# A layer stack on one core: weights, x and the scratch region moved onto 512-byte boundaries of each partition

## What is computed

```python
def _swiglu(h, w_gu, w_down):
    g, u = jnp.split(h @ w_gu, 2, axis=-1)
    return (jax.nn.silu(g) * u) @ w_down
...
x = x + 0.5 * _rmsnorm(_swiglu(_rmsnorm(x, ffn1_pre_g), ffn1_w_gu, ffn1_w_down), ffn1_post_g)
h = _rmsnorm(x, mix_pre_g)
q, k, v, z, xbc, dt_raw, gate_logits = jnp.split(h @ w_in, cuts, axis=-1)
...
mixed = (g_attn * attn_out + g_ssd * ssd_out) @ w_mix_out
x = x + _rmsnorm(mixed, mix_post_g)
```

## Time and profile before

| | |
|---|---|
| median of 3 runs | 1121.41 us (1120.94 to 1121.94) |
| profiled execution: time, span | 1121.69 us, 1119.9 us |
| TensorE busy | 1104.4 us, 99% |
| VectorE, ScalarE busy | 793.0 us, 590.9 us |
| granted clock | 1.00 |
| read from HBM | 186.50 MB |

### The profile page before, as it was taken

How to read it: one execution, slowest core, us unless ns; L and a number is a source line. 1 busy time by engine, 2 the same in 40 slices (tenths; PEclk the granted TensorE clock), 3 DMA queues, 4 the chain that set the end, 5 groups by cost and what they waited for, 6 DMA issues and landing times.

```text
span 1119.9 us, 20894 instructions
## 1 busy us (share of the span) xinstructions
PE 1104.4 (99%) x8484; PEld 1042.5 (93%) x8484; DVE 793.0 (71%) x1112; ACT 590.9 (53%) x844; POOL 0.2 (0%) x4
## 2 busy tenths in 40 slices
PE   9999999999999999999999999999999999999998
PEld 8999999999999999999999898999999799999998
DVE  5755555858898977777777867665555686987774
ACT  5444444557664325586744555443443575664561
POOL 0000000000000000000000000000000000000000
PEclk9999999999999999999999999999999999999999
DMA  8665555455544236444555434355555345543341
GB/s 298 241 222 187 190 184 188 168 183 180 185 151 148 94 136 207 155 147 151 188 174 177 169 114 160 131 200 206 173 176 206 128 166 198 184 151 114 114 151 38
DMA packets 29137, 188.59 MB, mean 168 GB/s; under 512 B 3496, under 2 KB 4809, under 8 KB 7370
## 3 DMA queue, kind: packets, MB, share of 16 engines
q1 hardware_dynamic: 26592, 181.42, 46.8%
q10 hardware_dynamic: 2474, 6.15, 1.7%
HBM read 186.50 MB, written 1.05 MB: 167 GB/s over the span
## 4 chain that ended last, share of the span: by engine, by line
PE 79%; DVE 15%; ACT 4%; issue 2%; DVEq 0%; ACTq 0%
PE bank L500 23%; PE bank L502 23%; PE bank L501 23%; DVE sb_w_lo L1973 4%; PE bank L581 2%; DVE sb_ssd_conv L2196 1%; ACT sb_w_hi L1287 1%; PE bank L816 1%; PE bank L961 1%; PE bank L655 1%; PE bank L1033 0%; PE bank L1012 0%; DVE sb_ssd_xdt L2243 0%; DVE sb_hyF L2626 0%; DVE sb_hyF L2625 0%
## 5 line engine op out<-in xcount | busy, mean ns | idle before, releaser
L1973 DVE TENSOR_TENSOR sb_w_lo<-sb_w_raw,sb_w_hi 128x2048 fp32r<-128x2048 f32 x169 | 386.5, 2290 | 156.9 <-ACT sb_w_hi L1287 156.7
L500 PE MATMUL bank<-sb_hT_hi,sb_w_hi 128*128 128x256 f32 x1560 | 442.7, 284 | 1.4 <-DVE sb_hT_lo L2050 1.3
L502 PE MATMUL bank<-sb_hT_hi,sb_w_lo 128*128 128x256 f32 x1560 | 435.3, 279 | 0.0
L501 PE MATMUL bank<-sb_hT_lo,sb_w_hi 128*128 128x256 f32 x1560 | 435.2, 279 | 0.0
L1287 ACT ACTIVATE sb_w_hi<-sb_w_raw 128x2048 fp32r<-128x2048 f32 x169 | 322.4, 1908 | 36.3 <-PE bank L502 34.9
L500 PEld LDWEIGHTS bank<-sb_hT_hi,sb_w_hi 128*128 128x128 f32 x1560 | 292.2, 187 | 6.0 <-issue 3.6
L501 PEld LDWEIGHTS bank<-sb_hT_lo,sb_w_hi 128*128 128x128 f32 x1560 | 291.8, 187 | 2.4 <-issue 1.2
L502 PEld LDWEIGHTS bank<-sb_hT_hi,sb_w_lo 128*128 128x128 f32 x1560 | 292.3, 187 | 0.0
L1341 ACT ACTIVATE sb_ffn_gate<-sb_ffn_gate 128x256 f32<-128x256 f32 x44 | 18.4, 418 | 140.7 <-DVE sb_ffn_gate L2065 140.7
L500 PE MATMUL bank<-sb_w_hi,sb_hT_hi 128*128 128x256 f32 x256 | 73.2, 286 | 0.6 <-DVE sb_hT_lo L2725 0.3
L501 PE MATMUL bank<-sb_w_lo,sb_hT_hi 128*128 128x256 f32 x256 | 71.1, 278 | 0.0
(11 more groups left out here) (431 smaller groups left out, 1751.3 us busy)
## 6 DMA issues: line engine op xcount, KB each, us to landing
sb_w_raw<-in_w SPq DMA_DIRECT2D x169, 1024.0 KB, 5.0
sb_x<-in_x SPq DMA_DIRECT2D x2, 512.0 KB, 4.6
sb_w_raw<-in_w SPq DMA_DIRECT2D x4, 256.0 KB, 7.0
sb_w_raw<-in_w SPq DMA_DIRECT2D x2, 512.0 KB, 8.2
sb_mem_xn<-in_mem ACTq DMA_DIRECT2D x1, 1024.0 KB, 7.8
sb_post_g<-in_ffn_post_g ACTq DMA_DIRECT2D x2, 512.0 KB, 4.6
sb_decay<-in_c_decay ACTq DMA_DIRECT2D x1, 768.0 KB, 4.3
out<-sb_x SPq DMA_DIRECT2D x3, 256.0 KB, 2.2
```

The costliest lines, as they stand in the source:

```text
L500: pe.matmul(o, a_hi, b_hi, start=first, stop=False)
L501: pe.matmul(o, a_hi, b_lo, start=False, stop=False)
L502: return pe.matmul(o, a_lo, b_hi, start=False, stop=last)
L1973: tt(w_lo[b % STAGES][:], w_raw[b % RING][:], f32(w_hi[b % STAGES][:]), ALU.subtract).then_inc(w_lo_in, 1)
```

## The change

Six small tensors are allocated ahead of the weights, `hT_hi` and `hT_lo` come right behind x, the other small tensors behind them, and 64 bytes that nobody uses (`to_row`) end the list. No instruction is added, removed or moved; each works on the same tensors at other addresses.

```diff
+ROW_GAP = 16
...
+        strict_r = sb("strict_r", [P, P], F32R)
+        newton = sb("newton", [P, 3, 16])
+        rstd = sb("rstd", [P, 16])
+        m_ssq = sb("m_ssq", [P, TOK * MLA_HEADS])
+        xr = sb("xr", [P, TOK])
+        xa_r = sb("xa_r", [P, TOK])
+
         w_raw = [sb(f"w_raw{i}", [P, BLOCK]) for i in range(RING)]
         w_hi = [sb(f"w_hi{i}", [P, BLOCK], F32R) for i in range(STAGES)]
         w_lo = [sb(f"w_lo{i}", [P, BLOCK], F32R) for i in range(STAGES)]
         x = sb("x", [P, TOK, D])
+        hT_hi = sb("hT_hi", [P, KD, SEQ], F32R)
+        hT_lo = sb("hT_lo", [P, KD, SEQ], F32R)
         square = sb("square", [P, 6 * P])
         cols = sb("cols", [P, NCOLS])
-        strict_r = sb("strict_r", [P, P], F32R)
         fcols = sb("fcols", [FILTER_HIDDEN, 4])
         rows = sb("rows", [P, NROWS])
         sub_g = sb("sub_g", [P, 1])
-        newton = sb("newton", [P, 3, 16])
         ssq = sb("ssq", [P, TOK])
...
-        m_ssq = sb("m_ssq", [P, TOK * MLA_HEADS])
-        rstd = sb("rstd", [P, 16])
-        xr = sb("xr", [P, TOK])
-        xa_r = sb("xa_r", [P, TOK])
         post_eps = sb("post_eps", [P, TOK])
-        hT_hi = sb("hT_hi", [P, KD, SEQ], F32R)
-        hT_lo = sb("hT_lo", [P, KD, SEQ], F32R)
+        sb("to_row", [P, ROW_GAP])
```

## The result

| | before | after |
|---|---|---|
| median of 4 runs each | 1121.53 us (1120.94 to 1121.94) | 1134.99 us (1134.89 to 1135.19) |
| ratio, 95% interval | | 1.0121 [1.0103, 1.0138] |
| profiled execution: time, span | 1121.69, 1119.9 us | 1134.89, 1133.1 us |

The forecast was 1109.5 us, with a range up to 1124.5. The time lies 13.5 us on the other side of before, and outside the range.

The account below looks back on a forecast made before the run. TensorE was taken to bound the kernel, with 79% of the chain. From the profiled 1121.69 us, 12 for faster split products and 0.1 for transfers gave 1109.6, against the median 1109.3; forecast 1109.5 us, range 1098 to 1124.5.

Parts of the forecast that it names:

- the bound of TensorE's split products: Split-product matmuls on TensorE: at best 23.6 us gained, at worst 6.6 us lost, nothing if only the starting phase decides.
- the value taken: Feature blocks get the token blocks' share of fast products, 68% for 9%: 14.1 us, 12 after losses where VectorE limits.
- The 512-column products: 528 products with 512 moving columns, left at 233.3 ns each; a gain, which nothing showed, would be 3.5 us.
- both operands on one footing is the worse footing: Rival: equal offsets make weight load and matmul collide, token blocks lose their fast cadence; 1125.7 to 1128 us, chance 0.23.
- The argument against it: Transposes of x have both operands alike within a row, yet last as long as the others.
- VectorE's 2290 ns: The 169 roundings on VectorE, mean 2290 ns each, were to stay unchanged.
- transfers: Loads hidden in the ring; only first x and last result could gain, 0.1 us taken, 0.4 at most.
- damped where other engines are the limit: Some 2 us of the products' gain lost where VectorE limits, 320 to 410 us and pauses at 900 us.
- the worse case: The layout makes split products slower: chance 0.23, of which a third was to stay below 1124.5 us.
- token blocks at 118 ns or a third cadence above it: Sign in the product starts that the change made the kernel worse, instead of feature blocks at 113.3 ns for 117.8.
- The rule of the Trainium skill: Loading next weights takes no read bandwidth from the running matmul, so their place wouldn't matter; only the ends' 0.1 us remains.

Follow-up runs that it names:

- e3: Kernel before with weights, hT and region all moved by 384 bytes, their offsets against each other unchanged: 1122.02 us, ratio 1.0001.
- e5: Kernel before with only a 448-byte pad ahead of hT_hi, operand offsets equal modulo 256, neither on a 512-byte boundary: 1134.84 us, ratio 1.0117.
- e1: Kernel before with pads that put weights and x on a 512-byte boundary, hT and region left at 448: 1112.91 us, ratio 0.9921.
- e4: Kernel before with only a 128-byte pad ahead of hT_hi, weights left at 128, hT and region at 64: 1115.15 us, ratio 0.9933.
- e7: e1 with the feed-forward halves that stand in 512-column blocks moved 64 bytes onto the weights' offset: 1119.28 us, ratio 0.9968 to the kernel before.
- m3_types: Matmul stretches without the layers, in three types at various operand offsets: float32 216 ns and bf16 109.2 ns at every offset; only fp32r varied.
- the map: Fp32r matmul stretches without the layers, each with other operand offsets: 256 columns took 120.0 ns at equal offsets, 113.3 and 117.8 at difference 192.

## Why the prediction was wrong

**The step that failed** is the bound of TensorE's split products: "Worst: all 1,475 products at the short cadence take the long one, 6.6 us more." It began with a true remark, that no row has both operands on a boundary, and then took the two cadences that the trace shows for the only ones there are. The trace had split products at D = 64 and 192 only; equal offsets give a third cadence, 120.0 ns, and it costs the 5,316 products of the long cadence too. Measured, the 256-column products cost 20.4 us more, where 6.6 had been called the worst.

**Its neighbour, the value taken,** failed with it. The 68% of the token blocks were read as "the moving operand lies better". e3 and e5 show that where an operand lies is nothing by itself. D = 192 for the feature blocks does make them faster: e1 has 66% of them short, near the token blocks' 68%, and its time falls by 8.6 us. But e4, with the same D, had 38% in its profile and e7 35%, so that the share came out is partly chance; and the layout that it was applied to had another D.

**The 512-column products,** "I leave them there", stood at 233.3 in all of the trace because it had one D for them. They fell to 227.9, 3.1 us of gain that the sum left out.

**The rival** *both operands on one footing is the worse footing* was the right mechanism at 0.23, mis-sized by the same bound: it priced only the loss of the short cadence, at 4.3 to 6.6 us, where the products cost 17.3 net and the time 13.5. The argument against it came from transposes in full precision, a type that m3_types shows to be indifferent.

**Right:** VectorE's 2290 ns; ScalarE; transfers, with landings of 4.9 and 4.4 us for 5.0 and 4.6, of which the 4.9 stands in e5 too, whose weights lie off the boundary; that a change in the products is damped where other engines are the limit. That was put at 2 us and was 4.1, 1.2 of them at the places named (320 to 410 us and around 900). Of what was to show the worse case the text named "token blocks at 118 ns or a third cadence above it", and it was the third cadence.

**The rule of the Trainium skill** that was weighed (TensorE: Matmul & The Clock Gate, Step-by-step: what each phase is for), by which loading the next weights takes nothing from the running matmul, would have given no change. The trace doesn't agree for fp32r: with 128 standing columns the map has 120.0 ns at D = 0 and 113.3 or 117.8 at D = 192, so where the two operands lie against each other does count. That it is the load and the running matmul that meet is the likely reading and not shown by itself. For bf16 and float32 no run here speaks against the rule.

**Left open:** which part of the memory or of its path the two share, and why by 256 bytes; no run here separates them. Nor was it found what at an entry picks one of the two cadences at D = 64 and 192. e7 shows that the block before it has a part in it, and e4 that this isn't all: behind the same block at the same D it is long where e1 is short.

## What to carry to other kernels

Where fp32r products bound a kernel, the offset of the moving operand against the standing one, modulo 256 bytes, is a setting of its own, worth 2% here between equal offsets and the best found (192 in the blocks where most products are); a pad of a few hundred bytes changes it, and "everything on a boundary" is a poor choice where 256 columns move. Measure it in the whole kernel and more than once, since a block's cadence depends on the one before it. And when a change makes an arrangement that no row of the trace has, the values seen so far are no bound on what it can cost.

## What the runs showed of the hardware

- The distance of back-to-back fp32r matmuls with 128 standing columns runs from 113.3 to 120.0 ns (256 moving columns) and from 226.7 to 234.3 (512) by D modulo 256, at multiples of 32 bytes (one stretch at D = 4 had 123.3, one at 16 had 118.7); bf16 stands at 109.2 and 215.9 ns, float32 at 216 and 429 for each of the two records of a product.
- At D = 64 and 192 there are two stable cadences, 113.3 and 117.8 ns, at the same addresses; D = 0 has one. A kernel with D = 0 repeats within 0.03% (1134.89 to 1135.19 us), one with D = 192 and 64 within 0.06% (e1, 1112.67 to 1113.35) or 0.6% (e4, 1112.37 to 1118.56).
- With 32 standing columns D = 0 and D = 448 give the same 113.3 ns; with 64 it is 113.4 at D = 0 and 119.0 at D = 192, the reverse of 128 columns, and with 96 it is 116.0 and 117.1. So which D is good depends on both widths.
- Faster products can cost part of their gain: in e1 TensorE waited 2.0 us for ScalarE, the granted clock then stood at 0.50, the 1.2 GHz level, and e1 lost 2.1 of its 11.4 us of lead over the kernel before. In e7 split products stood 213 ns apart at that level.
